# Two value projections with 512 weight columns per loaded token block instead of 256

## The reference, cut to what matters

```
# first block: stick-breaking attention
h = rmsnorm(x, pre_mix_g) * (1 + sc1) + sh1
proj = h @ w_in                                  # values: columns 2048:2560, 1024 x 512
o = stick_breaking_attention(q, k, v)
# second block: retention
h = rms_norm(x, attn_norm_w)
proj = h @ w_in                                  # values: columns 1024:1536, 1024 x 512
o = retention(rope(q), rope(k) / 8, v)
```

## Time and profile before

| | |
|---|---|
| median of 3 runs | 1400.73 us |
| lowest and highest | 1397.04 and 1400.82 us |
| span of the profiled execution | 1396.8 us |
| TensorE busy | 1342.1 us, 96% |
| TensorE weight loads busy | 1145.3 us, 82% |
| VectorE busy | 988.0 us, 71% |
| ScalarE busy | 694.5 us, 50% |
| GpSimd busy | 97.8 us, 7% |
| matmuls of the two value stages (L603) | 384 |

### The profile page before, as it was taken

One profiled execution on the slowest core, in us unless ns is written; L12 is line 12 of the kernel. 1 busy time (PEld: TensorE's weight loads), 2 busy tenths in 40 slices (PEclk: granted clock), 3 DMA queues, 4 the chain that ended last, 5 costly groups with the idle time before them and its releaser, 6 DMA issues. The chain is left out here.

```text
span 1396.8 us, 18640 instructions
## 1 busy us (share of the span) xinstructions
PE 1342.1 (96%) x7175; PEld 1145.3 (82%) x7175; DVE 988.0 (71%) x1230; ACT 694.5 (50%) x945; POOL 97.8 (7%) x73
## 2 busy tenths in 40 slices
PE   7999999999888999999999999989999999999997
PEld 4789888877567989998999897778878888888885
DVE  4899988777888749846848758878557745763663
ACT  4333777673345435533545755668355413441442
POOL 0000000011100193000012000000110000000001
PEclk9999999999999999999999999999999999999999
DMA  9544211147543423232251151210322232222221
GB/s 375 189 165 120 77 60 45 30 152 263 203 158 106 150 107 117 96 121 85 90 189 69 64 163 46 68 46 1 120 77 105 90 116 86 100 91 95 87 81 67
DMA packets 27894, 156.13 MB, mean 112 GB/s; under 512 B 3312, under 2 KB 3824, under 8 KB 14640
## 3 DMA queue, kind: packets, MB, share of 16 engines
q1 hardware_dynamic: 27824, 155.17, 31.7%
HBM read 145.98 MB, written 4.19 MB: 108 GB/s over the span
## 5 line engine op out<-in xcount | busy, mean ns | idle before, releaser
L1790 DVE TENSOR_TENSOR w_lo<-raw,w_hi 128x2048 fp32r<-128x2048 f32 (+3 forms) x135 | 254.4, 1885 | 86.0 <-ACT w_hi L1081 72.7
L1081 ACT ACTIVATE w_hi<-raw 128x2048 fp32r<-128x2048 f32 (+2 forms) x84 | 150.4, 1790 | 106.8 <-PE psum L606 62.7
L606 PE MATMUL psum<-h_hi,w_hi 128*128 128x512 f32 x376 | 96.4, 394 | 2.4 <-DVE w_lo L1790 2.1
L606 PE MATMUL psum<-h_hi,w_lo 128*128 128x512 f32 x376 | 95.1, 391 | 0.0
L606 PE MATMUL psum<-h_lo,w_hi 128*128 128x512 f32 x376 | 94.3, 389 | 0.0
L606 PEld LDWEIGHTS psum<-h_hi,w_hi 128*128 128x128 f32 x376 | 69.0, 188 | 18.3 <-DVE w_lo L1790 4.5
L606 PE MATMUL psum<-xg_hi,w_lo 128*128 128x512 f32 x336 | 83.0, 389 | 0.0
L606 PE MATMUL psum<-xg_lo,w_hi 128*128 128x512 f32 x336 | 83.0, 389 | 0.0
L606 PE MATMUL psum<-xg_hi,w_hi 128*128 128x512 f32 x336 | 83.0, 389 | 0.0
L606 PEld LDWEIGHTS psum<-h_lo,w_hi 128*128 128x128 f32 x376 | 70.6, 188 | 14.7
L606 PEld LDWEIGHTS psum<-h_hi,w_lo 128*128 128x128 f32 x376 | 70.0, 188 | 14.5
(11 more groups left out here) (415 smaller groups left out, 3047.5 us busy)
## 6 DMA issues: line engine op xcount, KB each, us to landing
raw<-w_ffn_in SPq DMA_DIRECT2D x22, 1024.0 KB, 4.9
raw<-w_up SPq DMA_DIRECT2D x22, 1024.0 KB, 4.8
ada_first<-ada SPq DMA_DIRECT2D x16, 512.0 KB, 11.6
raw<-w_gate SPq DMA_DIRECT2D x8, 1024.0 KB, 4.9
raw<-w_mix_out SPq DMA_DIRECT2D x8, 1024.0 KB, 5.5
raw<-w_ffn_out SPq DMA_DIRECT2D x8, 1024.0 KB, 4.9
raw<-w_down SPq DMA_DIRECT2D x8, 1024.0 KB, 4.8
ada_mid<-ada SPq DMA_DIRECT2D x11, 512.0 KB, 6.2
```

Of the source, the lines that this page charges most:

```text
L606: last = mm(ps, w[slot][:, k, t * P:(t + 1) * P], part(xv, k0 + k), start=first, stop=final)
L1081: A(w_hi[slot][:, 0:stage.kc, :], raw[slot][:, 0:stage.kc, :], ACT.Copy).then_inc(sem["w_hi_done"], 1)
L1790: return tt(out_lo, full, high.bitcast(F32), ALU.subtract)
```

## The change

The two value stages get a routine of their own, `row_blocks`. The two groups of weights no longer hold the two halves of the columns: they hold the two halves of K. Group s has chunks 4s to 4s+3 of K with all 512 columns, in the same 1 MB, and the host lays the weights out so. A matmul takes one loaded block of tokens and moves 512 weight columns, with 96 matmuls in a stage instead of 192, as many columns in all. Each of the four token blocks has a bank of its own (0 to 3), which stays open from the first half of K to the second. After the first half `tile_done` rises by two at once, which frees the first slot; the banks are complete only in the second half, two at its middle and two at its end. ScalarE's copies of the first half fall away; it reads the four banks, 512 columns each, behind the second group's preparations (`row_banks`). TensorE waits for the banks of the stage before in two steps (block 0 and block 2).

```
+            def row_blocks(stage, before):
+                for s in range(2):
+                    pe.wait_ge(sem["w_lo_done"], stage.g0 + s + 1)
+                    wide = [w[s][:, :, :].rearrange("p (k two) n -> p k (two n)", two=2) for w in (w_hi, w_lo)]
+                    for b in range(QB):
+                        if s == 0 and b % 2 == 0:
+                            pe.wait_ge(sem["group_free"], before + b // 2 + 1)
+                        for n, (w, xv) in enumerate(((wide[0], h_hi), (wide[1], h_hi), (wide[0], h_lo))):
+                            for k in range(4):
+                                last = mm(bank[b], xv[:, 4 * s + k, b * P:(b + 1) * P], w[:, k, :],
+                                          start=(s == 0 and n == 0 and k == 0), stop=(s == 1 and n == 2 and k == 3))
+                        if s == 0 and b == QB - 1:
+                            last.then_inc(sem["tile_done"], 2)
+                        elif s == 1 and b % 2 == 1:
+                            last.then_inc(sem["tile_done"], 1)
...
-            gemm(st["val"], h_hi, h_lo, rows=True)
+            row_blocks(st["val"], st["qk"].g0 + 2)
...
-            for k in range(2):
-                pe.wait_ge(sem["w_lo_done"], st["ret_val"].g0 + k + 1)
-                pe.wait_ge(sem["group_free"], rq.g0 + k + 1)
-                for t in range(2):
-                    tile(st["ret_val"], k, t, h_hi, h_lo, rows=True)
+            row_blocks(st["ret_val"], rq.g0)
...
-            def rows_of(stage, dst):
-                def evac(i, s, k, ahead):
-                    ahead()
-                    cols = slice(256 * k, 256 * k + 256)
-                    arrived(stage, k, 0)
-                    A(dst[:, 0:2, cols], bank[2 * s].rearrange("p (b n) -> p b n", b=2), ACT.Copy)
-                    arrived(stage, k, 1)
-                    free(stage, k, lambda: A(dst[:, 2:4, cols], bank[2 * s + 1].rearrange("p (b n) -> p b n", b=2), ACT.Copy))
-                return evac
+            def row_banks(stage, copy):
+                for b in range(QB):
+                    if b % 2 == 0:
+                        arrived(stage, 1, b // 2)
+                        copy(b)
+                    else:
+                        free(stage, b // 2, lambda: copy(b))
...
-                rows_of(st["val"], v_rows)(i, s, k, ahead)
+                ahead()
+                if k == 1:
+                    row_banks(st["val"], lambda b: A(v_rows[:, b, :], bank[b], ACT.Copy))
...
-                for b in range(QB):
-                    if b % 2 == 0:
-                        arrived(st["ret_val"], k, b // 2)
-                    copy = lambda: A(rv_rows[:, b, 256 * k:256 * k + 256], bank[2 * s + b // 2][:, b % 2 * 256:b % 2 * 256 + 256],
-                                     ACT.Copy, scale=rs_col[:, b:b + 1])
-                    if b < QB - 1:
-                        copy()
-                    else:
-                        free(st["ret_val"], k, copy)
+                else:
+                    row_banks(st["ret_val"], lambda b: A(rv_rows[:, b, :], bank[b], ACT.Copy, scale=rs_col[:, b:b + 1]))
...
+    for name in ("val", "ret_val"):
+        laid[name] = np.ascontiguousarray(out[name].reshape(2, 4, P, 512).transpose(0, 2, 1, 3).reshape(2, P, -1))
```

More of the change, by code:

```diff
@@ L589, in _, with tile @@
             PASSES = 3
-            def tile(stage, slot, t, x_hi, x_lo, k0=0, rows=False, ready=None, passes=range(PASSES)):
+            def tile(stage, slot, t, x_hi, x_lo, k0=0, passes=range(PASSES)):
                 ps, kc = bank[2 * slot + t], stage.kc
[L594 to L604, removed]
-                            else:
-                                last = mm(ps, w[slot][:, k, t * P:(t + 1) * P], part(xv, k0 + k), start=first, stop=final)
+                for n in passes:
+                    w, xv = ((w_hi, x_hi), (w_lo, x_hi), (w_hi, x_lo))[n]
+                    for k in range(kc):
+                        first, final = n == 0 and k == 0, n == PASSES - 1 and k == kc - 1
+                        last = mm(ps, w[slot][:, k, t * P:(t + 1) * P], part(xv, k0 + k), start=first, stop=final)
                 if passes[-1] == PASSES - 1:
@@ L627, in weights, with gemm @@
                     pe.wait_ge(sem["group_free"], g - 1)
-            def gemm(stage, x_hi, x_lo, k0=0, rows=False, ready=None, steps=None, beside=None):
+            def gemm(stage, x_hi, x_lo, k0=0, ready=None, steps=None, beside=None):
                 def group(i, s, first=False):
                     weights(stage.g0 + 2 * i + s)
-                    if first and ready and not rows:
+                    if first and ready:
                         first_group(stage, x_hi, x_lo, k0, ready, beside)
@@ L635, in group @@
                         for t in range(2):
-                            tile(stage, s, t, x_hi, x_lo, k0, rows, ready if first else None)
+                            tile(stage, s, t, x_hi, x_lo, k0)
                 begin, end = steps or (0, stage.n // 2)
```

## The result

The changed kernel takes 1403.38 us (median of 16 runs, 1399.68 to 1406.87), the kernel before in the same comparison 1400.28 us (16 runs, 1395.56 to 1402.51). The ratio is 1.0032, with a 95% interval of 1.0023 to 1.0041: slower, by just over the 0.3% that can be told from no change. The forecast was 1399.8 us, within 1395.6 to 1401.8: the time lies above that range. The profiled execution of after has a span of 1397.9 us, where before had 1396.8; at 1399.68 us it is the shortest of the 16, so the profile shows less than the typical loss.

What follows compares the result with a forecast made beforehand. The prediction took TensorE, busy 1342.1 of 1396.8 us, as the bound unless another engine ends last. Gains of 0 (attention) and 0.93 us (retention) took the median from 1400.73 to 1399.8 us, range 1395.6 to 1401.8.

Steps and rivals of the forecast that it cites:

- The price of the matmuls: Both value stages: 96 wide matmuls at 226.7 ns take 21.76 us, 1.27 us less TensorE work per stage.
- The attention's stage: Attention's value stage: 1.27 us off TensorE, but gain 0, because VectorE's full list sets the time.
- `t_lo` comes when it came: Attention, head 0: VectorE's list is unchanged, so the input TensorE waits for arrives at its old time; gain 0.
- which come at 128.36 by a DMA: Attention: ScalarE's keys were taken to arrive at 128.36 us, as before, without waiting for the value matmuls.
- just in time: Attention: the gate weights' low part ends at 136.8 us, when the scores end at the earliest.
- not 1.85: Attention, head 0: TensorE's wait for `t_lo` was to grow from 0.58 to about 1.85 us, at no cost.
- The retention's stage: Retention's value stage: 1.27 us off TensorE, of which 0.93 us off the time; bounds 0 and 1.27.
- the 0.24: Retention: 0.24 us of the 1.27 goes into a new TensorE wait for VectorE's last `pair` ahead of the scores.
- the 0.10: Retention: the eight scores take 0.10 us more behind a wait, 1.31 against 1.21 us.
- ScalarE's wide copies: Retention: four 512-column PSUM copies take 2.06 us instead of 1.54, costing only above about 0.65 us each.
- Slower, by the clock: Rival, chance 0.10: the clock falls behind head 0's longer wait, costing up to 1.75 us; 1401.6 us.
- The fall at 930 us goes: Rival, chance 0.10: the clock fall at 930 to 940 us disappears, saving 1.75 us; 1398.0 us.

Runs made afterwards that it cites:

- e3: Kernel before with only the attention's value stage changed to the wide form: 1402.2 us (5 runs), ratio 1.0043.
- e4: Kernel before with only the retention's value stage changed to the wide form: 1399.18 us (11 runs), ratio 1.0010.
- e2: The changed kernel, unedited, measured and profiled again: 1403.57 us (4 runs) against 1397.17, ratio 1.0050.
- e12: The changed kernel plus eight filler matmuls behind the attention's value stage: 1401.11 us (8 runs), ratio 1.0036.
- e7: The changed kernel with the first gate and latent weight loads issued ahead of the key copies: 1396.67 us (12 runs), ratio 0.9993 to the kernel before.
- e1: The kernel before, unedited, profiled once more: 1399.08 us in one run.
- e9: Kernel before with first gate and latent loads ahead of the key copies, and 512-column matmuls in the retention's value stage alone: 1395.29 us (11 runs), ratio 0.9985.
- e11: The changed kernel with a tiny DMA between the attention's second key copy and the gate load: 1402.11 us (4 runs), ratio 1.0040.
- e5: The changed kernel with each 512-column matmul split into two of 256, all else kept: 1397.78 us (10 runs), ratio 0.9999 to the kernel before.
- e6: Kernel before with ScalarE's first-group PSUM copies moved behind the second group's preparations: 1398.25 us (10 runs), ratio 1.0007.
- e8: Kernel before with the first gate and latent weight loads issued ahead of the key copies: 1396.11 us (12 runs), ratio 0.9988.

## Why the prediction was wrong, point by point

**The price of the matmuls: right.** The stages take 21.76 us, as worked out from 226.7 ns; each is 1.27 us shorter. The rows of the other orientation held. The rule of the Trainium skill, "TensorE: Matmul & The Clock Gate", section "Back-to-back issue gap", would have taken only 0.24 us off a stage; the trace doesn't bear it out here, with 1.27 us.

**The attention's stage: right in that nothing is gained, wrong in that nothing is lost.** By the times this is the costlier failure: e3, with this stage alone, is at 1.0043, and e4, with the other alone, at 1.0010. The step that failed is "`t_lo` comes when it came", together with the keys "which come at 128.36 by a DMA". VectorE's list is unchanged, but a list with no slack is also one on which every late input counts. The text itself had the gate weights' low part as "just in time", at 136.8: cover nil. The keys' lateness of 2.9 us in after (2.7 from the first issue) used up what ScalarE had in hand, 15.47 - 13.66 = 1.8 us, and cost 0.86 us more; in e2, e12 and e3 it cost 1.35 to 2.23, and in e2 and e3 the clock fell behind it for another 1.55 and 2.9. The term that the prediction put at 0 was a loss. The wait was 2.24 us, not 1.85; in e7, where the keys are early, it is 1.84.

**The retention's stage: the same step failed.** The prediction saw that `pair` "hangs on a DMA of the keys that lands at 816.07 [...], not on TensorE", and took 816.07 as fixed, since weight DMAs are "as large and as many, issued in the same order". Size, number and order did stay; the landing did not. It came 3.9 us later, 2.8 of them counted from the first issue, and the new wait was 2.48 us instead of 0.24. Between the two first profiles the term of -0.93 us became +1.43. Part of that is the early landing in before's one profile, taken for a constant: e1 has 7.9 us instead of 5.8 with nothing changed, and against e1 the wide stage of e2 comes out even. What all wide profiles beside late loads show is that nothing of the 0.93 us is gained. With the copy out of the way (e9) the gain is 1.29 us, above the forecast's 0.93, since then neither the 0.24 nor the 0.10 arises.

**ScalarE's wide copies.** They took 2.43 us for four instead of the 2.06 assumed, within the bound of the text (0.65 each), and no wait of `latent` for them shows.

**The rivals.** "Slower, by the clock" did happen, in its place and near its size: 1.55 us in e2, 1.56 in e7, against 1.75 worked out. But it can't be the whole cause: the fall at 146 to 155 us is absent from the profiles of after, e11 and e12, and e12 is slow with TensorE kept busy there. How much falls of the clock elsewhere cost is open (above). Its condition was too simple: among the profiles with a wait of 1.84 to 2.24 us in head 0 the clock fell in e2, e3 and e7 and held in after and e11; with waits of 0.57 or 0.58 us (before, e1, e4, e5, e6, e8, e9) it held in all seven. Ahead of the retention's scores it held behind 2.48 us in after and fell behind 3.05 in e4. By the rule of the Trainium skill in "TensorE: Matmul & The Clock Gate", section "Part 1: The HAM clock gate", an idle array is what drops to the half clock. The 0.50 of e3, behind a wait of 2.23 us, agrees; the length of the wait alone didn't decide here. "The fall at 930 us goes" happened too, in after, where it gave back 2.56 - 1.04 = 1.52 us.

**The range.** It left out the one case that came: a loss through a transfer that the change doesn't touch by name. No rival had the DMA's landing time in it, though both stages' steps ended on it.

## What to carry to other kernels

A DMA row's landing time is not a constant of the kernel: where a step ends on a transfer that shares its queue with large loads, price it a few microseconds late as well, and look at a second execution before trusting it. Taking work off TensorE is worth nothing while its next input hangs on such a transfer; move the transfer first (here one weight load issued earlier). In the stage that TensorE bounds, the wide matmuls then paid in full in e9's profile. Where another engine bounds, they paid nothing here, and e7, which has them there too, had a fall of the clock behind the longer wait. That the narrow form is the better choice in such a place is argued from this: the times of e7 (0.9993), e8 (0.9988) and e9 (0.9985) don't separate clearly.

## What the runs showed of the hardware

- The width of TensorE's moving operand went with the time of DMAs on their way at the same moment: in the attention the third copy of 512 KB took 9.2 to 10.7 us beside 512-column matmuls (8.3 in e11, behind a tiny DMA) and 6.5 to 7.7 beside 256-column ones with the same transfers issued in the same order, and the 1 MB loads around it 11.8 to 12.6 us instead of 8.1 to 9.5. With the weight load out of the way the copy took 4.2 us in either case. In the retention narrow matmuls did not prevent 9.2 and 10.7 us (e5, e3).
- An issue on SyncE's queue held it for about 2 us instead of 0.6, and in the attention it differed with the width of the matmuls beside it which of the issues that was.
- A wait of TensorE of 1.84 us stood ahead of a fall of its granted clock in one execution (0.86 and 0.80 in two stretches of 5 us), and a wait of 2.24 us did not in another.
- A fall of the clock ahead of idle time of TensorE cost little or nothing: after had 0.69 at 926 to 931 us and was 1.5 us less late behind it than ahead of it, against before, whose fall came later, from 930 to 940 us.
